# The last depths of two projections, multiplied in another order: two depths converted early and passed over

## What is computed

```python
y = jnp.concatenate([ya, yb, yc], axis=-1) @ w_out[l]     # 2048 x 2048: the output projection
x = x + rms_norm(y, post_mix_g[l])
h = rms_norm(x, pre_mlp_g[l])
u = jnp.square(jax.nn.relu(h @ w_up[l])) @ w_down[l]      # up: 2048 x 8192, down: 8192 x 2048
x = x + rms_norm(u, post_mlp_g[l])
```

## Time and profile before

| what | value |
|---|---|
| device time, median of 3 | 1334.19 us (1332.52 to 1335.41) |
| the profiled execution's own time | 1333.89 us |
| its span, first to last instruction | 1332.1 us |
| PE busy | 1294.0 us, 97% |
| DVE busy | 814.6 us, 61% |
| ACT busy | 646.0 us, 48% |
| POOL busy | 304.3 us, 23% |
| read from HBM | 222.69 MB, 169 GB/s over the span |

### The profile page before, as it was taken

How to read it: one execution, slowest core, us unless ns; L and a number is a source line. 1 busy time by engine, 2 the same in 40 slices (tenths; PEclk the granted TensorE clock), 3 DMA queues, 4 the chain that set the end, 5 groups by cost and what they waited for, 6 DMA issues and landing times.

```text
span 1332.1 us, 25395 instructions
## 1 busy us (share of the span) xinstructions
PE 1294.0 (97%) x10525; PEld 1138.5 (85%) x10525; DVE 814.6 (61%) x1131; ACT 646.0 (48%) x992; POOL 304.3 (23%) x255
## 2 busy tenths in 40 slices
PE   6999999999999999998999999999999999999996
PEld 5999888888899898877888888888888888888885
DVE  5556778777776977457555555555555555555555
ACT  5465664566434457447444444444444444444443
POOL 0011333234205130000555554555520000000000
PEclk9999999999999999999999999999999999999998
DMA  8656433332357445873766666666666666666663
GB/s 256 188 169 177 121 107 97 97 96 82 109 128 202 122 123 155 285 208 107 226 190 189 190 189 190 189 190 190 190 190 193 194 195 191 193 196 193 191 193 109
DMA packets 285752, 226.44 MB, mean 170 GB/s; under 512 B 15237, under 2 KB 263301, under 8 KB 284741
## 3 DMA queue, kind: packets, MB, share of 16 engines
q1 hardware_dynamic: 285168, 223.57, 57.4%
q0 software_dynamic: 240, 1.18, 0.3%
q10 hardware_dynamic: 228, 0.07, 0.0%
HBM read 222.69 MB, written 2.10 MB: 169 GB/s over the span
## 4 chain that ended last, share of the span: by engine, by line
PE 67%; DVE 3%; ACT 1%; issue 1%; DMA 0%; DVEq 0%; ACTq 0%
PE psum L2132 32%; PE psum L1751 18%; PE psum L1762 9%; PE psum L1735 2%; PE psum L1741 2%; PE psum L1736 2%; DVE w_lo L778 1%; ACT w_hi L1331 0%; DMA raw<-in_w_out 0%; PE psum L2187 0%; PE psum L2108 0%; DVE spare L778 0%; PE psum L2010 0%; PE psum L2100 0%; PE psum L1897 0%
## 5 line engine op out<-in xcount | busy, mean ns | idle before, releaser
L778 DVE TENSOR_TENSOR w_lo<-raw,w_hi 128x1024 fp32r<-128x1024 f32 x394 | 497.4, 1265 | 402.2 <-ACT w_hi L1331 401.4
L1331 ACT ACTIVATE w_hi<-raw 128x1024 fp32r<-128x1024 f32 x394 | 418.6, 1066 | 458.2 <-PE psum L2132 214.4
L2132 PE MATMUL psum<-w_hi,act_both 128*128 128x512 f32 x1216 | 328.3, 391 | 3.6 <-DVE act_both L1284 2.7
L2132 PEld LDWEIGHTS psum<-w_hi,act_both 128*128 128x128 f32 x1216 | 228.6, 188 | 52.3 <-DVE act_both L1284 3.1
L1751 PE MATMUL psum<-act_both,w_hi 128*128 128x512 f32 x1024 | 246.6, 391 | 0.0
L1735 PE MATMUL psum<-act_both,w_hi 128*128 128x256 f32 x912 | 239.6, 296 | 1.8 <-issue 1.4
L1736 PE MATMUL psum<-act_both,w_hi 128*128 128x256 f32 x912 | 227.2, 283 | 0.0
L1751 PEld LDWEIGHTS psum<-act_both,w_hi 128*128 128x128 f32 x1024 | 188.1, 188 | 36.5
L2132 PE MATMUL psum<-w_lo,act_both 128*128 128x512 f32 x608 | 187.7, 390 | 0.0
L1735 PEld LDWEIGHTS psum<-act_both,w_hi 128*128 128x128 f32 x912 | 173.6, 190 | 10.2 <-issue 3.1
L1736 PEld LDWEIGHTS psum<-act_both,w_hi 128*128 128x128 f32 x912 | 174.2, 191 | 0.1
(11 more groups left out here) (234 smaller groups left out, 1051.2 us busy)
## 6 DMA issues: line engine op xcount, KB each, us to landing
raw<-in_w_up SPq DMA_DIRECT2D x128, 512.0 KB, 4.1
raw<-in_w_down SPq DMA_DIRECT2D x128, 512.0 KB, 4.4
raw<-in_w_in SPq DMA_DIRECT2D x114, 512.0 KB, 4.2
raw<-in_w_out SPq DMA_DIRECT2D x32, 512.0 KB, 4.6
arena<-in_x SPq DMA_DIRECT2D x2, 1024.0 KB, 6.3
arena<-in_na_rpb SPq DMA_DIRECT2D x16, 128.0 KB, 4.5
arena<-in_x SPq DMA_DIRECT2D x1, 2048.0 KB, 8.4
out_x<-arena SPq DMA_DIRECT2D x4, 512.0 KB, 2.7
```

The lines of the kernel that those rows point to most:

```text
L778: dve.tensor_tensor(by_half(h, low(h)), by_pair(h, raw[:, h % RAW]), by_half(h, high(h)).bitcast(F32), ALU.subtract).then_inc(s["lo_half"], 1)
L1331: act.activation(by_half(h, high(h)), by_pair(h, raw[:, h % RAW]), ACT.Copy).then_inc(s["hi_half"], 1)
L2132: last = pe.matmul(bank[4 * t + 2 * j + b], lhs[:, tokens], w[:, b * 512:(b + 1) * 512], start=start, stop=stop)
```

## The change

The halves are fetched and converted in the same order as before. What changes is which of them lie in the spare slots, and the order in which PE multiplies the last five depths:

- Output projection: PE multiplied depths 0 to 12 in turn and then held 13, 14, 15. Now it multiplies 0 to 10, passes over 11 and 12, multiplies 13 and 14, and holds 15, 11, 12 in that order. Depths 11 and 12 (halves 136 to 139) are in the spare slots; 13, 14, 15 (halves 140 to 145) are in the ring.
- Down: 0 to 58, then 61 and 62, and held are 63, 59, 60. Depths 59 and 60 (halves 392 to 395) are in the spare slots, halves 396 to 401 in the ring.
- `slot_free` gets the counts that belong to this: six numbers for the last six halves, and for the first three halves of up, half 146 waits for the depths multiplied in turn, and 147 and 148 for `held_free`.
- The split activations of depths 59 and 60 get two places of their own beside the ring of four (`u_slot`, `u_slot_free`), which are free all through down.

```diff
@@ -192,7 +192,7 @@
         w_lo = sb("w_lo", [P, SPLIT, HALF], F32R)
         act_both = sb("act_both", [P, KT, 2, T], F32R)
         act_hi, act_lo = act_both[:, :, 0], act_both[:, :, 1]
-        u_hi, u_lo = act_hi[:, 0:U_RING], act_lo[:, 0:U_RING]
+        u_hi, u_lo = act_hi[:, 0:U_RING + HELD - 1], act_lo[:, 0:U_RING + HELD - 1]
         cst = sb("cst", [P, CST_N])
         vec = sb("vec", [P, VEC_N])
         small = sb("small", [P, 256])
@@ -476,12 +476,34 @@
             return bass.AP(tensor=tokens.tensor, offset=tokens.offset + last * (count - 1),
                            ap=steps[:-1] + [[-last, count]])
 
+        def from_end(h):
+
+            return h - next(end for end in (OUT_H, UP_H, DOWN_H, END_H) if h < end) if h >= OUT_H else -END_H
+
         def spare_slot(h):
 
-            for end in (UP_H, END_H):
-                if end - 2 * HELD + 2 <= h < end:
-                    return h - (end - 2 * HELD + 2)
+            if OUT_H <= h < UP_H or h >= DOWN_H:
+                at = from_end(h) + 4 * HELD - 2
+                if 0 <= at < 2 * HELD - 2:
+                    return at
             return None
+
+        def depth_order(count):
+
+            early = list(range(count - 2 * HELD + 1, count - HELD))
+            return [n for n in range(count - 1) if n not in early], [count - 1] + early
+
+        def u_slot(m):
+            return m % U_RING if m not in depth_order(FF_T)[1][1:] else U_RING + m - depth_order(FF_T)[1][1]
+
+        def u_slot_free(eng, m):
+
+            if m < U_RING:
+                eng.wait_ge(s["gemm_half"], DOWN_H - 1)
+            elif m in depth_order(FF_T)[1]:
+                eng.wait_ge(s["gemm_half"], DOWN_H + 2 * (FF_T - 2 * U_RING))
+            else:
+                eng.wait_ge(s["gemm_half"], DOWN_H + 2 * (m - U_RING) + 2)
 
         def high(h):
             return w_hi[:, h % SPLIT] if spare_slot(h) is None else spare_hi[:, spare_slot(h)]
@@ -494,10 +516,12 @@
             if spare_slot(h) is not None:
                 eng.wait_ge(s["gemm_half"], h - 2 * HELD - 2)
                 eng.wait_ge(s["y_lo"], KT)
-            elif UP_H <= h < UP_H + 2:
-                eng.wait_ge(s["held_free"], h - UP_H + 1)
-            elif h == UP_H + 2:
+            elif h == UP_H:
                 eng.wait_ge(s["gemm_half"], UP_H - 2 * HELD)
+            elif UP_H < h < UP_H + 3:
+                eng.wait_ge(s["held_free"], h - UP_H)
+            elif (OUT_H <= h < UP_H or h >= DOWN_H) and from_end(h) >= -2 * HELD:
+                eng.wait_ge(s["gemm_half"], h - from_end(h) - (11, 10, 12, 9, 8, 7)[from_end(h) + 2 * HELD])
             elif h >= SPLIT:
                 eng.wait_ge(s["gemm_half"], h - SPLIT + 1)
 
@@ -1281,7 +1305,7 @@
 
             def u_rest(m):
                 dve.wait_ge(s["uhi_done"], m + 1)
-                dve.tensor_tensor(u_lo[:, m % U_RING], u[:, m], u_hi[:, m % U_RING].bitcast(F32),
+                dve.tensor_tensor(u_lo[:, u_slot(m)], u[:, m], u_hi[:, u_slot(m)].bitcast(F32),
                                   ALU.subtract).then_inc(s["ulo_done"], 1)
 
             lo(DOWN_H)
@@ -1686,8 +1710,8 @@
 
             def u_split(m):
                 act.wait_ge(s["relu_free"], 3 + m // 2)
-                act.wait_ge(s["gemm_half"], DOWN_H - 1 if m < U_RING else DOWN_H + 2 * (m - U_RING) + 2)
-                act.activation(u_hi[:, m % U_RING], u[:, m], ACT.Copy).then_inc(s["uhi_done"], 1)
+                u_slot_free(act, m)
+                act.activation(u_hi[:, u_slot(m)], u[:, m], ACT.Copy).then_inc(s["uhi_done"], 1)
 
             hi(DOWN_H)
             u_split(0)
@@ -2176,12 +2200,12 @@
                         elif final:
                             last.then_inc(s["gemm_half"], 2 * HELD)
 
-            for n in range(KT - HELD):
+            in_turn, held = depth_order(KT)
+            for n in in_turn:
                 pe.wait_ge(s["y_lo"], n + 1)
                 rows(OUT_H // 2 + n, act_hi[:, OUT_ORDER[n]], act_lo[:, OUT_ORDER[n]], n == 0)
             pe.wait_ge(s["y_lo"], KT)
-            held_rows([(OUT_H // 2 + n, act_hi[:, OUT_ORDER[n]], act_lo[:, OUT_ORDER[n]])
-                       for n in range(KT - HELD, KT)])
+            held_rows([(OUT_H // 2 + n, act_hi[:, OUT_ORDER[n]], act_lo[:, OUT_ORDER[n]]) for n in held])
 
             def turn_x1(k, t):
                 return pe.transpose(norm_place(k)[:, t * P:(t + 1) * P], x1[:, t, k * P:(k + 1) * P], ident)
@@ -2222,12 +2246,12 @@
                     up_low(b, h + 1, late)
                     up_high(b, h + 1, late, stop=True).then_inc(s["gemm_half"], 1)
 
-            for m in range(FF_T - HELD):
+            in_turn, held = depth_order(FF_T)
+            for m in in_turn:
                 pe.wait_ge(s["ulo_done"], m + 1)
-                rows(DOWN_H // 2 + m, u_hi[:, m % U_RING], u_lo[:, m % U_RING], m == 0)
+                rows(DOWN_H // 2 + m, u_hi[:, u_slot(m)], u_lo[:, u_slot(m)], m == 0)
             pe.wait_ge(s["ulo_done"], FF_T)
-            held_rows([(DOWN_H // 2 + m, u_hi[:, m % U_RING], u_lo[:, m % U_RING])
-                       for m in range(FF_T - HELD, FF_T)])
+            held_rows([(DOWN_H // 2 + m, u_hi[:, u_slot(m)], u_lo[:, u_slot(m)]) for m in held])
 
 
 _INS = ("x", "pre_mix_g", "w_in", "na_rpb", "rw_mu_prev", "rw_mu_next", "rw_w0", "rw_w2", "rw_a0", "rw_a2", "rw_k_k",
```

## The result

| | median us (range, executions) | ratio to before, 95% interval | profiled execution, span, mean clock |
|---|---|---|---|
| before | 1335.08 (1332.52 to 1335.46, 7) | | 1333.89, 1332.1, 0.995 |
| changed | 1341.24 (1338.09 to 1343.29, 7) | 1.0046 [1.0036, 1.0056] | 1338.09, 1336.3, 0.994 |

The changed kernel is slower, by 6.2 us. The forecast was 3.9 us, a time of 1338.1 and a range of 1335.3 to 1339.8: **the direction and the places were right, the size was too small, and the time lies above the range.** Of the 3.1 us between 1338.1 and 1341.24, 2.3 are the effect's; the rest is the base, since before has a median of 1335.08 over seven executions where the prediction had 1334.19 over three. The execution that was profiled took 1338.09 us, just the forecast, but it is the fastest of the seven. That coincidence hides the error from whoever looks at one trace only.

What follows compares the result with a forecast made beforehand. PE was taken as the bound, busy 97% of the span, with the conversion leading by only 2.9 us. Output projection 2.0, down 0.2 and clock 1.7 summed to +3.9 us, giving 1338.1, range 1335.3 to 1339.8.

Steps and rivals of the forecast that it cites:

- the base: Whole kernel: the profiled execution's 1333.89 us plus 3.9 gives 1337.8; as it lies 0.3 below the median, 1338.1.
- The jump in the output projection: Output projection: PE needs half 140 four halves sooner and gets it 3.0 us late, plus 0.13 for the next six matmuls.
- the transfer of half 140: Output projection, on the path to the jump: issued at 571.95, taken as 5.0 us because four transfers follow in quick succession.
- rival B: Both jumps: bunched transfers slow each other to 6.1 us, stalls grow to about 4.2 us, together +6.3, 1340.5; chance 0.09.
- The old wait as a credit: Output projection: the wait for late half 145 goes, saving 1.07 us and leaving net +2.0 there.
- The clock: The new output projection stall lowers the clock, +1.7 us; in down one fall replaces another, 0.
- rival A: Both new stalls: only one lowers the clock, 1336.4 (chance 0.22), or neither, 1334.7 (0.05); gaps near the longest harmless one.
- The turn to up: Between output projection and up: nothing hangs on the changed waits of halves 146 and 147, the late chain is the same; 0.
- Down: End of down: half 396 comes 3.05 us late, the old 2.85 us wait goes; net +0.2, only a change of place.
- the two upper bounds: Stall terms: output projection +2.0 could reach 3.2, down +0.2 could reach +1.5.

Runs made afterwards that it cites:

- before_again: The kernel before the change, run once more with no edit for a second trace: 1334.47 us, ratio 1.0010 to before.
- after: The changed kernel itself, in its first set of seven executions: 1341.24 us, ratio 1.0046 to before.
- after_again: The changed kernel run a second time with no edit, ten executions: 1340.28 us, ratio 1.0044 to before.
- after_third: The changed kernel run a third time with no edit, two executions: 1341.12 us, ratio 1.0056 to before.
- out_only: The change in the output projection alone, with down as in the kernel before: 1340.24 us, ratio 1.0042 to before.
- fifth_raw: The changed kernel plus a fifth raw buffer in down, from half 380 on: 1336.92 us, ratio 1.0017 to before.
- filler: The changed kernel plus 12 extra matmuls ahead of the wait at each of the two jumps: 1336.77 us, ratio 1.0019 to before.
- jump_one_placed: Before with per-depth waits for the split of u and a one-depth jump in down, halves 394 to 397 in spare slots: 1330.89 us, ratio 0.9970.
- jump_one: Before with per-depth waits for the split of u and a one-depth jump in down, half 396 in the ring: 1332.66 us, ratio 0.9994.

## Why the prediction was too low

The end of the output projection, by trace; the last five jump over two depths there. The third column is the output end as above, the fourth runs from the first transpose of the turn to the first matmul of up.

| trace | idle at the jump | output end | turn | low clock at the jump / the turn |
|---|---|---|---|---|
| before_again | none | | 8.84 | none / 3.4 |
| after | 2.83 | 28.69 | 8.84 | 3.4 / 3.4 |
| after_again | 3.86 | 29.68 | 9.77 | 6.8 / 6.8 |
| after_third | 3.41 | 28.92 | 10.03 | 3.4 / 6.8 |
| out_only | 3.22 | 30.17 | 10.03 | 6.8 / 6.8 |
| fifth_raw | 3.67 | 28.94 | 7.89 | 3.4 / none |

**The jump in the output projection.** The mechanism held to the step: nothing on PE's path is late but the round half 136, raw buffer, half 140, and ACT waits for the transfer. The size was short in most executions. The prediction had PE 3.0 us late plus 0.13; the mean idle time of the five is 3.40, and PE starts 0.16 later than that counts: 3.56, or +0.4. The mis-sized part is the transfer of half 140: I took 5.0 for it, and it takes 4.93, 5.96, 5.51, 5.32 and 5.76 in the five, mean 5.5. That is rival B: not another way for all executions to go, but what some of them do.

**The old wait as a credit.** This is the step that failed clearly. I took off 1.07 us for a wait of 0.78 that the profiled execution showed. Of five other traces of the same output projection three have nothing of it and two 0.4 and 0.3 us, so the mean credit over six is 0.3: +0.8.

**The clock.** It fell where I put a fall: rival A had 0.27 for one stall or both leaving it alone, and of the five traces with this jump none did (the unprofiled execution of 1333.58 us may have, by its mean clock). But the term 1.7 was the price of one short stretch. The output end exceeds 27.20 by 1.5, 2.5, 1.7, 3.0 and 1.7: mean 2.1, +0.4. In each of these traces the clock is low for either 3.4 or 6.8 us. The reason that I gave for A had little behind it: after the first microseconds, the longest idle time of PE that left the clock alone in the trace of before is 1.4 us, at 19.6 us; only later traces show longer ones.

**The turn to up.** I had it at 0, "which is the same". Its chain of work is the same, its clock isn't: 8.84 in before, and 0, 0.93, 1.19, 1.19 and -0.95 more in the five, mean +0.5. The edit doesn't touch it. Of seven traces without this jump, and with no extra matmuls at the turn, six take 8.84 there and one 7.89, none more. Why the turn is longer in three of the five I haven't shown; it may be that only the moment at which PE stops there has moved.

**Down.** Stall moved, not gained, as said: the down end is 35.58, 35.42, 35.77 and 35.55 in the traces that have the jump there, 35.17, 35.04 and 35.24 where not. +0.4 for the forecast +0.2. PE resumed 3.26 us late in `after` (due 1295.68, 1298.94), forecast 3.05.

**The sum.** 3.56 - 0.3 + 2.1 + 0.5 = 5.9 for the output projection, which `out_only` measured as 5.75 by itself; with 0.4 for down 6.3, measured 6.2. My 3.9 was short by 0.4 + 0.8 + 0.4 + 0.5 + 0.2 = 2.3. These means rest on five traces for 35 executions, among them the slowest of ten (`after_again`) and the fastest of seven (`after`), so that the sum fits to 0.1 us is partly luck.

**The base and the range.** Adding to one execution made both errors one-sided: it had the rare wait to give credit for and the short stretch to price. I left out B with 1340.5 and a chance of 0.09. The transfer of 6.1 us was in my bound for the output projection (4.1 + 0.13 - 1.07 = 3.2), but the two upper bounds added to the forecast, 1.2 and 1.3 us, give 1340.6, and the range stopped at 1339.8. What it should have carried beside them is the credit's absence (+1.07) and a longer low stretch.

**What is open.** What decides whether the clock falls and for how long. A PE idle for 3.55 us at the turn keeps the full clock in `filler`, `fifth_raw` and `jump_one_placed` and loses it elsewhere; 2.56 us in `jump_one` leave it alone, 2.69 in the earlier trace rows don't. In the stretches of 6.8 us the clock fell 0.75 us or more before PE resumed (`out_only` and `after_again` at the jump, these and `after_third` at the turn), in those of 3.4 at the earliest 0.5 us before. That is a pattern over these traces, no test. A fifth raw buffer for the output projection wasn't tried.

## What to carry to other kernels

Before data is converted early into spare places and passed over in the multiply order, compare the converters' lead with the jump: here the lead is 2.9 us and a jump over two depths needs 10.9, so the first half behind it comes a whole round of a raw buffer after the first one converted early (7.3 us in `after`, from 572.34 to 579.64), of which PE had to wait 3.0; where it stays in a ring, its ring place must be long free as well. Ask first whether the wait to be removed covers more than its consumer needs: making it finer brought 5.2 us of the 5.6 that the reordering was after (4.5 of them seen in the down end), and took two lines. Don't credit an edit in full with removing a wait of under 1 us that one trace shows, and price a fall of the clock by more than one.

## What the hardware showed that I had not expected

- The low clock lasts 3.4 or 6.8 us, in the same place of the same kernel; it costs 1.5 to 3.0 us behind a jump. The turn, with 3.5 us of waiting inside, takes 7.89 us at full clock, 8.84 with the short and 9.8 to 10.0 with the long stretch.
- Filling an idle PE with matmuls that serve nothing saved 3.4 us net in `filler`.
- The same transfer, in a steady stream 2.72 us apart, takes another time from execution to execution. From 1230 to 1270 us, in `after` and then in `after_again`, the same kernel (min/median/max):

```profile
DMA to landing us min/median/max: 3.5/3.6/4.4
```

```profile
DMA to landing us min/median/max: 4.2/4.4/5.4
```

- Near 560 us, behind the load of `x` (transfers there take 7.7 to 13 us), seven of the fourteen traces show another wait of PE, of 0.7 to 1.8 us: 1.6 in `after_again`, where the half that PE waits for took 12.95 us to land, none in `after`, `after_third` or the two traces of before. The change has not yet set in there, so it is a source of spread that it has no part in.
